# Second attention: the last item's probabilities multiplied before the new item's maxima on VectorE

## The chip, the cores and the metric

The kernel runs on one core of a Trainium2 chip. The time is device microseconds of one execution of the whole program. Of the kernel before there are three timed runs, with a median of 1680.32 us (1678.73 to 1683.52), and one profiled execution. TensorE is PE in the rows, VectorE DVE, ScalarE ACT, GpSimd POOL.

## What is computed

Two transformer blocks in float32 on one sequence of 512 tokens, width 1024. The first block has a retention mixer, an RWKV7 mixer, a cross attention and an MLP. The second block has four mixers beside each other, of four heads of 64 each, and a convolutional feed-forward part. The change is in the second block, in three of its four mixers, which the kernel computes in one stage:

```python
# diff attention: two softmaxes a head, subtracted
p = jax.nn.softmax(s, axis=-1)
w = p[:, :, 0] - lam * p[:, :, 1]
o = einsum('bhqk,bhkd->bhqd', w, v)
# forgetting attention: s + (cq[..., :, None] - cum[..., None, :]), causal
p = jax.nn.softmax(s, axis=-1)
# native sparse attention: three branches on one q, compressed keys (31),
# selected keys, window keys; each softmax(q k + bias) v, times its gate
o = g[:, 0] * o_c + g[:, 1] * o_s + g[:, 2] * o_w
```

The fourth, stick breaking attention, is done in the stage before.

## The kernel before, in words

Every engine has its program written out by hand, one function for each engine and stage, and waits on semaphores. The dense products (L389) run before and after the stage; inside it there are only four blocks of a last one, in steps 0 to 1, and nothing else is there to fill TensorE.

`mixer_items` lists 40 **items**. An item is one tile of 128 queries (t is 0 to 3) for a pair of heads, with keys up to w = 128 (t + 1). Items 0 to 15 are diff items (four **maps**: two softmaxes for two heads) and fox items (two maps) in the order d d f d f d f f, twice, with t = 3, 0, 2, 1 for each kind. Items 16 to 39 are the sparse attention, two maps each, in triples of one t (3, 0, 2, 1, twice): the compressed keys (w = 31), the selected and the window keys (w = 128 to 512).

A loop over n, the **step**, stands in each engine's function:

- TensorE, `mixers_pe`: `scores(n)` (L2406, one matmul a map into one of four PSUM banks, which waits until VectorE has read that bank four maps earlier); then `turn(n - 2)` (L2418, transposes of the probabilities, which wait for them and for the PSUM bank that ScalarE's `keep(n - 3)` empties); then `times_v(n - 3)` (L2431).
- VectorE, `mixers_dve`: `front(n)` (L2474, for each map one pass that adds the bias to the scores, writes them negated to a ring of 8 slots in SBUF and accumulates the minimum; it waits for the scores, for the transposes that read the slot before, and for the fox bias), then `back(n - 1)` (L2481 a reciprocal of the sums; L2483 a mask for w = 31; L2490 and L2495 the four multiplies of a diff item; L2502 or L2504 two multiplies of the others), which waits for the exponentials of item n - 1.
- ScalarE, `mixers_act`: `exps(n)` (L2526, one exponential a map with its sum, after that map's minimum), then `keep(n - 2)` (L2535, the transposed probabilities from PSUM to SBUF), now and then `keep_out(n - 4)` (L2541) and work for the next stage (`beside_mixers_act`: L2782, L2788, L2792).
- GpSimd, `fox_bias_pool`: the biases of the eight fox items (L2571, L2573), two fox items ahead.

So in one step VectorE takes the maxima of item n and afterwards multiplies the probabilities of item n - 1, whose exponentials ScalarE computed in the meantime. Four items are in flight. The small subtractions of `beside_mixers_dve` (L2807, four of them) stand at the end of a step.

Of the kernel before, what the change touches and what calls it, by code (L numbers as in the profile page):

```python
# [160 lines left out]
def build_program(nc, A, out):  # L161

    ctx = ExitStack()
    with ctx:
# [182 lines left out]
        def fill(steps, n):  # L347

            for _ in range(n):
                next(steps, None)  # L350
# [67 lines left out]
        def evac_steps(side, me, chunks):  # L418

            for ch in chunks:  # L420
                ahead = ch["index"] + 1
                while ahead < len(STREAM) and STREAM[ahead].get("kind"):
                    ahead += 1
                split_weights(side, me, ahead)
                if me == "dve" and ch.get("kind") == "modulation":
                    add_modulation(side, ch)
                for b in ch["blocks"]:
                    if units_of(b) == 2:
                        yield
                    if b["last"] and b["owner"] == me:  # L430
                        side.wait_ge(acc_done, b["acc"])
                        b["evac"](side, ps[0:b["m"], b["bank"], 0:b["n"]], bank_free[me], b["free"])
                    elif b["last"] and b["other"]:
                        b["other"](side, bank_free[b["owner"]], b["free"])
                    yield
# [1881 lines left out]
        def ring(j):  # L2317

            return yT[:, j, :] if j < 4 else SRING[:, j % 8, :]
# [71 lines left out]
        MIX = mixer_items()  # L2391
# [69 lines left out]
        def mixers_dve(v):  # L2461

            def front(it):
                for k, (_, _, bias) in enumerate(it["maps"]):
                    j = it["j0"] + k
                    v.wait_ge(mx_scores, j + 1)
                    if j >= 12:

                        v.wait_ge(mx_turned, 2 * MAP_ITEM[j - 8]["n"] + 2)
                    if it["kind"] == "fox":  # L2470
                        v.wait_ge(fox_bias, 2 * it["fox"] + k + 1)
                    r = j % 8

                    nc.vector.tensor_tensor_reduce(  # L2474
                        out=ring(j)[:, 0:it["w"]], in0=ps[:, j % 4, 0:it["w"]], in1=bias, scale=-1.0, scalar=3.0e38,
                        op0=ALU.add, op1=ALU.min, accum_out=MINS[:, r:r + 1]).then_inc(mx_shifted, 1)

            def back(it):
                n_maps, w, r, j0 = len(it["maps"]), it["w"], it["j0"] % 8, it["j0"]
                v.wait_ge(mx_exp, it["j0"] + n_maps)  # L2480
                nc.vector.reciprocal(RECS[:, r:r + n_maps], SUMS[:, r:r + n_maps]).then_inc(dve_order, 1)  # L2481
                if it["valid"] is not None:
                    nc.vector.tensor_tensor(SRING[:, r:r + 2, 0:w], SRING[:, r:r + 2, 0:w], it["valid"],  # L2483
                                            ALU.mult).then_inc(dve_order, 1)
                    v.count(dve_order)
                v.wait_ge(dve_order, v.count(dve_order))
                if it["kind"] == "diff":
                    for e in range(2):
                        p1 = ring(j0 + 2 + e)[:, 0:w]
                        nc.vector.tensor_scalar(p1, p1, RECS[:, r + 2 + e:r + 3 + e], NEG_LAM, ALU.mult,  # L2490
                                                ALU.mult).then_inc(dve_order, 1)
                    for e in range(2):
                        p = ring(j0 + e)[:, 0:w]
                        v.wait_ge(dve_order, v.count(dve_order))
                        nc.vector.scalar_tensor_tensor(out=p, in0=p, scalar=RECS[:, r + e:r + e + 1],  # L2495
                                                       in1=ring(j0 + 2 + e)[:, 0:w], op0=ALU.mult,
                                                       op1=ALU.add).then_inc(mx_probs, 1)
                    return
                for e in range(2):
                    p, rec = ring(j0 + e)[:, 0:w], RECS[:, r + e:r + e + 1]  # L2500
                    if it["gate"]:
                        ins = nc.vector.tensor_scalar(p, p, rec, it["gate"][e], ALU.mult, ALU.mult)  # L2502
                    else:
                        ins = nc.vector.tensor_scalar(p, p, rec, None, ALU.mult)  # L2504
                    ins.then_inc(mx_probs, 1)

            dense = evac_steps(v, "dve", v_tail)
            fill(dense, 1)
            for n in range(len(MIX) + 1):
                if n < len(MIX):  # L2510
                    front(MIX[n])
                if n:
                    back(MIX[n - 1])
                if n < 2:
                    fill(dense, n + 1)
                beside_mixers_dve(v, n)
# [286 lines left out]
        def beside_mixers_dve(v, n):  # L2803
            if n - 2 in MIX_SPLIT:
                k = MIX_SPLIT[n - 2]
                v.wait_ge(split_high, v.count(split_high))
                nc.vector.tensor_tensor(Y_LOW[:, k - 2, :], yT[:, k, :], Y_HIGH[:, k - 2, :].bitcast(F32),  # L2807
                                        ALU.subtract).then_inc(split_low, 1)
# [330 lines left out]
        @block.vector  # L3139
        def _(eng):  # L3140
            v = Side(eng, stage_sem)
            v.split = 0
            start_dve(v)
            front1_dve(v)
            invert_dve(v)
            v.stage_end()
            grams_dve(v)
            v.stage_end()
            scan_dve(v)
            v.stage_end()  # L3150
            w_out_dve(v)
            w_qkv_dve(v)
            v.stage_end()
            cross_dve(v)
            w_o_dve(v)
            mlp_dve(v)
            front_dve(v)
            mixers_dve(v)
            w_out_2_dve(v)
            evac_products(v, "dve", ffn)  # L3160
# [68 lines left out]
```

## Time and profile before

| what | value |
|---|---|
| three timed runs, median | 1680.32 us |
| the profiled execution, its own time | 1683.01 us |
| its span | 1681.2 us |
| PE busy, share of the span | 1610.1 us, 96% |
| DVE busy | 889.3 us, 53% |
| ACT busy | 660.7 us, 39% |
| POOL busy | 102.3 us, 6% |
| mean granted clock of TensorE | 0.991 |
| the stage with the 40 items | from 1151.9 to 1264 us of the span |

The profile is of one execution. Busy time is the time in which an engine had an instruction under way; TensorE's matmuls overlap, so a busy TensorE need not be at its peak. A release time is inferred from semaphores: behind a row, `[1.88 <-PE ps L2406]` says that the engine was idle for 1.88 us until an instruction of PE on line 2406 ended.

### The profile page before, as it was taken

The page shows a single profiled execution, that of the slowest core. Times are in us where ns is not written, and L with a number is a line of the kernel's source. Part 1 is how long each engine was busy: PE and PEld are TensorE (multiplying, and loading weights), DVE is VectorE, ACT ScalarE, POOL GpSimd, SP SyncE. Part 2 cuts the span into 40 slices and gives each one's busy share as a digit, 9 for nine tenths or more (in the row PEclk, how much of TensorE's full clock was granted, in tenths as well). Part 3 has the DMA queues.
Part 4 walks back from the last instruction along what each step waited for, and adds up shares of the span by engine and source line. Part 5 has one row for each costly group of instructions (what it writes and reads, how often), then busy time and mean ns, then how long its engine had stood idle before and what let it go on. Part 6 is the DMA issues. An engine that isn't in the chain of part 4 may idle for free.

```text
span 1681.2 us, 26254 instructions
## 1 busy us (share of the span) xinstructions
PE 1610.1 (96%) x11335; PEld 1288.7 (77%) x11335; DVE 889.3 (53%) x1384; ACT 660.7 (39%) x990; POOL 102.3 (6%) x125
## 2 busy tenths in 40 slices
PE   7999987899999999999999999999889999999998
PEld 5866767878896778888888778786558788888887
DVE  6454584516445364555455644537775655555544
ACT  3215932143534354333241334656774522222220
POOL 1300115000000000000000100003200000000000
PEclk9999999999999999999999999999899999999999
DMA  6612120005242345536453442321003233333222
GB/s 212 178 51 75 54 84 4 4 28 184 91 151 76 125 130 161 190 109 217 125 191 133 152 130 61 76 76 51 3 13 89 75 101 100 101 100 92 88 86 87
DMA packets 150694, 170.32 MB, mean 101 GB/s; under 512 B 14296, under 2 KB 111202, under 8 KB 150194
## 3 DMA queue, kind: packets, MB, share of 16 engines
q1 hardware_dynamic: 142424, 156.82, 29.6%
q10 hardware_dynamic: 8154, 11.81, 2.5%
q8 instruction: 90, 1.47, 0.4%
q14 instruction: 26, 0.21, 0.0%
HBM read 164.12 MB, written 6.33 MB: 101 GB/s over the span
## 4 chain that ended last, share of the span: by engine, by line
PE 83%; DVE 6%; ACT 5%; issue 2%; DMA 1%; POOL 1%; ACTq 0%; SPq 0%; DVEq 0%; POOLq 0%
PE ps L389 66%; PE ps L1255 3%; PE ps L1435 2%; DVE weights_low L412 1%; PE ps L2406 1%; PE ps L2418 1%; DMA sb_arena<-sb_arena 1%; PE ps L2431 1%; PE ps L2614 1%; PE ps L1661 1%; ACT sb_hT L2526 1%; PE ps L895 1%; PE ps L907 1%; ACT weights_high L409 1%; ACT sb_arena L672 1%
## 5 line engine op out<-in xcount | busy, mean ns | idle before, releaser
L389 PE MATMUL ps<-left_high,weights_high 128*128 128x512 f32 (+1 forms) x1016 | 404.1, 398 | 8.3 <-DVE left_low L694 3.1
L412 DVE TENSOR_TENSOR weights_low<-sb_weights_raw,weights_high 128x2048 fp32r<-128x2048 f32 (+1 forms) x118 | 265.2, 2248 | 258.2 <-ACT weights_high L409 258.1
L389 PE MATMUL ps<-left_low,weights_high 128*128 128x512 f32 (+1 forms) x1016 | 396.4, 390 | 0.0
L389 PE MATMUL ps<-left_high,weights_low 128*128 128x512 f32 (+1 forms) x1016 | 396.3, 390 | 0.0
L409 ACT CAST weights_high<-sb_weights_raw 128x2048 fp32r<-128x2048 f32 (+1 forms) x118 | 221.4, 1877 | 324.3 <-PE ps L389 282.7
L389 PEld LDWEIGHTS ps<-left_high,weights_high 128*128 128x128 f32 (+1 forms) x1016 | 190.3, 187 | 64.1 <-issue 13.2
L389 PEld LDWEIGHTS ps<-left_high,weights_low 128*128 128x128 f32 (+1 forms) x1016 | 190.5, 187 | 41.0
L389 PEld LDWEIGHTS ps<-left_low,weights_high 128*128 128x128 f32 (+1 forms) x1016 | 190.6, 188 | 40.4 <-issue 1.7
L389 PE MATMUL ps<-weights_high,hidden_high 128*128 128x512 f32 x432 | 169.0, 391 | 0.0
L389 PE MATMUL ps<-weights_high,hidden_low 128*128 128x512 f32 x432 | 168.2, 389 | 0.0
L389 PE MATMUL ps<-weights_low,hidden_high 128*128 128x512 f32 x432 | 168.1, 389 | 0.0
L389 PE MATMUL ps<-weights_high,left_high 128*128 128x256 f32 (+2 forms) x320 | 105.4, 329 | 1.6 <-DVE weights_low L412 1.2
L389 PE MATMUL ps<-weights_low,left_high 128*128 128x256 f32 (+2 forms) x320 | 103.9, 325 | 0.0
L389 PE MATMUL ps<-weights_high,left_low 128*128 128x256 f32 (+2 forms) x320 | 103.9, 325 | 0.0
L389 PEld LDWEIGHTS ps<-weights_high,hidden_low 128*128 128x128 f32 x432 | 81.1, 188 | 17.2
L389 PEld LDWEIGHTS ps<-weights_high,hidden_high 128*128 128x128 f32 x432 | 81.1, 188 | 16.7
L389 PEld LDWEIGHTS ps<-weights_low,hidden_high 128*128 128x128 f32 x432 | 81.1, 188 | 16.5
L1874 DVE TENSOR_TENSOR hidden_low<-sb_arena,hidden_high 128x512 fp32r<-128x512 f32 x54 | 37.3, 691 | 89.3 <-ACT hidden_high L1869 89.3
L389 PEld LDWEIGHTS ps<-weights_high,left_high 128*128 128x128 f32 x320 | 60.8, 190 | 10.5 <-issue 2.7
L389 PEld LDWEIGHTS ps<-weights_low,left_high 128*128 128x128 f32 x320 | 60.8, 190 | 5.5 <-issue 0.5
L389 PEld LDWEIGHTS ps<-weights_high,left_low 128*128 128x128 f32 x320 | 60.8, 190 | 5.1
L451 DVE SCALAR_TENSOR_TENSOR sb_arena<-sb_yT,sb_derived_cols,sb_arena 128x512 f32<-128x512 f32 x84 | 63.1, 751 | 3.0
(408 smaller groups left out, 2135.0 us busy)
## 6 DMA issues: line engine op xcount, KB each, us to landing
sb_weights_raw<-in_w_in SPq DMA_DIRECT2D x25, 1024.0 KB, 5.3
sb_yT<-in_ada_w SPq DMA_DIRECT2D x24, 1024.0 KB, 5.2
sb_weights_raw<-in_ffn_w_up SPq DMA_DIRECT2D x44, 512.0 KB, 5.0
sb_weights_raw<-in_mlp_w_up SPq DMA_DIRECT2D x16, 1024.0 KB, 6.2
sb_weights_raw<-in_mlp_w_down SPq DMA_DIRECT2D x16, 1024.0 KB, 7.8
sb_weights_raw<-in_ffn_w_down SPq DMA_DIRECT2D x10, 1024.0 KB, 5.0
sb_weights_raw<-in_xattn_w_kv SPq DMA_DIRECT2D x8, 1024.0 KB, 5.2
sb_weights_raw<-in_w_out SPq DMA_DIRECT2D x6, 1024.0 KB, 5.0
```

What stands on the lines that cost most here:

```text
L389: last = nc.tensor.matmul(o, lhsT, rhs, start=b["first"] and i == 0, stop=b["last"] and i == len(pairs) - 1)
L409: nc.scalar.copy(h[:, 0:n], raw[:, 0:n]).then_inc(w_high, 1)
L412: nc.vector.tensor_tensor(l[:, 0:n], raw[:, 0:n], h[:, 0:n].bitcast(F32), ALU.subtract).then_inc(w_low, 1)
L451: nc.vector.scalar_tensor_tensor(out=MOD_ACC, in0=w[:, k], scalar=C_ACT[:, kt:kt + 1], in1=MOD_ACC, op0=ALU.mult, op1=ALU.add).then_inc(do ...
L672: nc.scalar.activation(nm["shifted"][:, k, :], ps[:, k, :], ACT.Identity, scale=nm["gain"](k), bias=nm["shift"](k)).then_inc(norm_shifted, 1)
L895: nc.tensor.matmul(ps[:, 2 + n % 4, 0:w], KTt[b, p_, kt * P:(kt + 1) * P], QT[b, p_, kt * P:S], start=True, stop=True).then_inc(ret_scores, 1)
L907: last = nc.tensor.matmul(ps[64 * e:64 * e + 64, 6 + p_ % 2, kt * P:S], VR[:, kt, h * 64:(h + 1) * 64], SCO[:, (s - 2) % 3, e, 0:w], start ...
L1255: last = nc.tensor.matmul(ps[to, bank, c * 64:(c + 1) * 64], lhsT(b, u, c), rhs(b, u, c), start=True, stop=True)
L1435: last = nc.tensor.matmul(o_of(b), *own_pairs[i], start=i == 0, stop=i == len(own_pairs) - 1)
L1661: last = nc.tensor.matmul(ps[b, 6 + o % 2, q0:S], v_of(x), PT[0:m, buf, x, q0:S], start=grp["begins"] and x == 0, stop=grp["ends"] and x = ...
L1874: nc.vector.tensor_tensor(HIDL[part % 2][:, i, :], x, HIDH[part % 2][:, i, :].bitcast(F32), ALU.subtract).then_inc(ff_low, 1)
L2406: nc.tensor.matmul(ps[:, j % 4, 0:it["w"]], l, r, start=True, stop=True).then_inc(mx_scores, 1)
```

## The change

In VectorE's loop the two calls change places. From step 1 on, `back(n - 1)` comes first, and `front(n)` after it. Nothing else is changed: no instruction is added, removed or altered, and the programs of the other four engines are the same, row for row.

```diff
             for n in range(len(MIX) + 1):
+                if n:
+                    back(MIX[n - 1])
                 if n < len(MIX):
                     front(MIX[n])
-                if n:
-                    back(MIX[n - 1])
                 if n < 2:
                     fill(dense, n + 1)
                 beside_mixers_dve(v, n)
```

VectorE's order at the first sparse triple, before. ISA is the pass of `front` (128x512: selected or window keys of the last query tile; 128x31: compressed keys), the rows 128x1 its accumulator. The first rows are the maxima of item 17 (selected keys); the words in brackets are the semaphores that a row waits for.

```order
L2474 ISA sb_hT,sb_stat<-ps,sb_arena 128x512 [waits mix_probs_turned,mix_scores]
L2474 ISA sb_stat 128x1
L2481 RECIPROCAL sb_stat<-sb_stat 128x2 [waits mix_exp_ready]
L2483 TENSOR_TENSOR sb_hT<-sb_hT,sb_arena 128x2x31
L2502 TENSOR_SCALAR sb_hT<-sb_hT,sb_stat,sb_arena 128x31 [waits dve_order]
L2502 TENSOR_SCALAR sb_hT<-sb_hT,sb_stat,sb_arena 128x31
L2474 ISA sb_hT,sb_stat<-ps,sb_arena 128x512 [waits mix_probs_turned,mix_scores]
L2474 ISA sb_stat 128x1
L2474 ISA sb_hT,sb_stat<-ps,sb_arena 128x512 [waits mix_probs_turned,mix_scores]
L2474 ISA sb_stat 128x1
L2481 RECIPROCAL sb_stat<-sb_stat 128x2 [waits mix_exp_ready]
L2502 TENSOR_SCALAR sb_hT<-sb_hT,sb_stat,sb_arena 128x512 [waits dve_order]
```

The same place in the changed kernel:

```order
L2483 TENSOR_TENSOR sb_hT<-sb_hT,sb_arena 128x2x31
L2502 TENSOR_SCALAR sb_hT<-sb_hT,sb_stat,sb_arena 128x31 [waits dve_order]
L2502 TENSOR_SCALAR sb_hT<-sb_hT,sb_stat,sb_arena 128x31
L2474 ISA sb_hT,sb_stat<-ps,sb_arena 128x512 [waits mix_probs_turned,mix_scores]
L2474 ISA sb_stat 128x1
L2474 ISA sb_hT,sb_stat<-ps,sb_arena 128x512 [waits mix_probs_turned,mix_scores]
L2474 ISA sb_stat 128x1
L2481 RECIPROCAL sb_stat<-sb_stat 128x2 [waits mix_exp_ready]
L2502 TENSOR_SCALAR sb_hT<-sb_hT,sb_stat,sb_arena 128x512 [waits dve_order]
L2502 TENSOR_SCALAR sb_hT<-sb_hT,sb_stat,sb_arena 128x512
L2474 ISA sb_hT,sb_stat<-ps,sb_arena 128x512 [waits mix_probs_turned,mix_scores]
L2474 ISA sb_stat 128x1
```

Before, the reciprocal that waits for item 16's exponentials stood behind the maxima of item 17; now the maxima of item 17 are followed at once by the reciprocal that waits for the exponentials of item 17 itself, and the maxima of item 18 stand behind it.

## Rows read from the trace of the kernel before

**Rows 1.** Busy time in two stretches: items 2 to 15, items 16 to 39; columns: stretch, length, then per engine busy (instructions), then PEclk, DMA

```profile
1162.30:1206.60 44.30, 38.57 (x284) 23.96 (x282) 37.20 (x136) 32.66 (x109) 20.57 (x27) 0.85 0.00 1
1206.60:1262.30 55.70, 48.66 (x402) 29.77 (x402) 39.49 (x184) 43.30 (x159) 0.00 (x0) 0.97 0.04 11
```

**Rows 2.** Waits, 1162.3 to 1262.3 us: total, times, longest

```profile
ACT sb_hT L2526 <- DVE sb_stat L2474: 28.4, 25, 5.8
DVE sb_hT L2474 <- PE ps L2406: 17.4, 21, 3.0
```

**Rows 3.** Timeline of DVE, item 18's maxima and item 17's multiplies: start, length

```profile
1211.99 0.69 DVE L2474 CUSTOM_DVE_ANT_0 sb_hT<-ps,sb_arena 128x512 f32<-128x512 f32 x1 [0.40 <-PE ps L2406]
...
1212.61 0.69 DVE L2474 CUSTOM_DVE_ANT_0 sb_hT<-ps,sb_arena 128x512 f32<-128x512 f32 x1
...
1213.22 0.16 DVE L2481 RECIPROCAL sb_stat<-sb_stat 128x2 f32<-128x2 f32 x1
1213.42 1.00 DVE L2502 TENSOR_SCALAR sb_hT<-sb_hT,sb_stat,sb_arena 128x512 f32<-128x512 f32 x2
1214.33 0.20 DVE L2474 CUSTOM_DVE_ANT_0 sb_hT<-ps,sb_arena 128x31 f32<-128x31 f32 x1
```

**Rows 4.** Timeline of ACT, the exponentials of item 18

```profile
1212.73 0.72 ACT L2526 ACTIVATE sb_hT<-sb_hT,sb_stat 128x512 f32<-128x512 f32 x1
...
1213.45 0.70 ACT L2526 ACTIVATE sb_hT<-sb_hT,sb_stat 128x512 f32<-128x512 f32 x1
1214.06 0.18 ACT L2526 ACTIVATION_READ_ACCUMULATOR sb_hT<-sb_hT,sb_stat 128x1 f32 x1
```

**Rows 5.** Groups of instructions by line, 1162.3 to 1262.3 us: count, busy, mean ns, idle before

```profile
L2526 ACT ACTIVATE sb_hT<-sb_hT,sb_stat 128x384 f32<-128x384 f32 (+4 forms) x88 | 44.8, 511 | 28.7 <-DVE sb_stat L2474 28.4
L2474 DVE CUSTOM_DVE_ANT_0 sb_hT<-ps,sb_arena 128x384 f32<-128x384 f32 (+4 forms) x72 | 27.7, 422 | 18.4 <-PE ps L2406 15.9 <-PE ps L2418 1.7 <-issue 0.4
...
L2502 DVE TENSOR_SCALAR sb_hT<-sb_hT,sb_stat,sb_arena 128x31 f32<-128x31 f32 (+4 forms) x48 | 16.9, 394 | 0.9
...
L2495 DVE SCALAR_TENSOR_TENSOR sb_hT<-sb_hT,sb_stat 128x128 f32<-128x128 f32 (+3 forms) x14 | 7.5, 575 | 0.0
...
L2490 DVE TENSOR_SCALAR sb_hT<-sb_hT,sb_stat,sb_derived_cols 128x128 f32<-128x128 f32 (+3 forms) x14 | 6.9, 531 | 0.3
L2481 DVE RECIPROCAL sb_stat<-sb_stat 128x2 f32<-128x2 f32 (+1 forms) x39 | 6.3, 162 | 0.0
...
L2504 DVE TENSOR_SCALAR sb_hT<-sb_hT,sb_stat 128x512 f32<-128x512 f32 (+3 forms) x16 | 5.5, 384 | 0.3
...
L2483 DVE TENSOR_TENSOR sb_hT<-sb_hT,sb_arena 128x62 f32<-128x62 f32 x8 | 1.6, 202 | 0.0
```

**Rows 6.** Timeline of ACT, a copy for TensorE's next users, and DVE, which waits for it

```profile
1405.25 0.62 ACT L1869 CAST hidden_high<-sb_arena 128x512 fp32r<-128x512 f32 x1 [2.70 <-DVE sb_arena L2864]
...
1405.97 0.69 DVE L1874 TENSOR_TENSOR hidden_low<-sb_arena,hidden_high 128x512 fp32r<-128x512 f32 x1 [0.76 <-ACT hidden_high L1869]
```

**Rows 7.** Timeline of DVE: last dense block, item 1's multiplies, end of the last item

```profile
1161.34 0.42 DVE L475 COPY sb_arena<-ps 128x256 f32<-128x256 f32 x1 [2.24 <-PE ps L389]
...
1163.62 0.17 DVE L2481 RECIPROCAL sb_stat<-sb_stat 128x4 f32<-128x4 f32 x1
...
1165.16 0.55 DVE L2474 CUSTOM_DVE_ANT_0 sb_hT<-ps,sb_arena 128x384 f32<-128x384 f32 x1
...
1261.45 0.73 DVE L2502 TENSOR_SCALAR sb_hT<-sb_hT,sb_stat,sb_arena 128x256 f32<-128x256 f32 x2
```

**Rows 8.** Timeline of ACT in step 31, from its copies after the exponentials

```profile
1240.48 1.04 ACT L2535 COPY sb_hT<-ps 128x512 f32<-128x512 f32 x2
...
1241.89 1.07 ACT L2788 ACTIVATE sb_arena<-sb_yT 128x1024 f32<-128x1024 f32 x1
```

**Rows 9.** Timeline of PE: eight transposes at granted clock 0.5, and at 1.0

```profile
1187.60 1.93 PE L2418 MATMUL ps<-sb_consts,sb_hT 128*128 128x128 f32 x8
...
1216.32 1.09 PE L2418 MATMUL ps<-sb_consts,sb_hT 128*128 128x128 f32 x8
```

## The prediction

> **What bounds the kernel now.** I began with the page: TensorE is busy for 96% of the span, nearly all of it dense products, and none of these is touched. So the change can only be worth what it does to the stage of the 40 items. Next came the busy time by stretch [rows 1]. From item 2 to item 39 the stage takes 100.0 us, and no engine fills it: PE 87.2 (38.57 + 48.66), DVE 76.7 (37.20 + 39.49), ACT 76.0 (32.66 + 43.30). A stage in which three engines are each busy for three quarters or more and none all the time is bound by how they wait for each other. The waits say how [rows 2]: DVE stands idle 21 times, 17.4 us in all, for the scores of TensorE, and ACT 25 times, 28.4 us, for the maxima of DVE. No row has DVE waiting for ACT's exponentials. That absence is what the present order buys: when DVE comes to multiply item n - 1, it has just spent the maxima of item n on something else, and the exponentials are ready.
>
> The round trip through TensorE is the one that shows. Multiplies of item n - 2 release its transposes, behind these and behind times_v(n - 3) stand the scores of item n + 1 in TensorE's queue, and DVE needs them two steps later.
>
> **What the change does.** It changes no instruction, only DVE's order. The multiplies of item n - 1 come one front earlier, so the transposes, and with them the next scores, come earlier: the 17.4 us of waiting for scores should go. In return DVE now goes from the last maximum of item n - 1 straight to a reciprocal that needs the sum of item n - 1's last exponential, and the maxima of item n are queued behind that reciprocal. ACT cannot start item n's exponentials before those. DVE and ACT thus work in turn, and a closed loop arises with one item in it:
>
> first maximum of item n, then all its exponentials on ACT, then the way back to DVE, then the multiplies of item n, then the first maximum of item n + 1.
>
> Only the first maximum counts, since ACT is the slower of the two: at 512 columns an exponential takes 0.72 and 0.70 us [rows 4] and the second maximum starts 0.62 after the first [rows 3]. For an item of two maps and 512 columns the loop costs: from the start of the maximum (1211.99) to the exponential (1212.73) 0.74; exponentials to the end of the accumulator read (1214.24) 1.51; the way from ACT to DVE; reciprocal and multiplies (1213.22 to 1214.33) 1.11 [rows 3, 4]. The way from ACT to DVE is not shown in this stage, since DVE never waits there. Its nearest row is in the feed-forward part: a copy ends at 1405.87 and DVE starts at 1405.97 [rows 6]; I take 0.10, with 0.05 to 0.15 as the ends. That makes 3.46 us for the item.
>
> **The sum over items 2 to 39** (38 items, 88 maps) goes by the grouped rows [rows 5]:
>
> - Exponentials: 44.8 us, all 88 of them, and the tail of the last accumulator read of each item, 0.10 x 38 = 3.8. Together 48.6.
> - Way to DVE: 0.10 x 38 = 3.8.
> - First maxima: one for each item; the mean of a map is 0.42, the items of 128 to 512 columns weigh it up to 0.43, and 0.04 follows until ACT starts: 0.47 x 38 = 17.8. The other 50 maxima are hidden behind exponentials.
> - Reciprocals and multiplies: 16.9 + 7.5 + 6.9 + 6.3 + 5.5 + 1.6 = 44.7. Off this go item 1's, 1.54 (1163.62 to 1165.16, [rows 7]), and 0.07 an item, by which a multiply's end overlaps the next start (0.16 + 1.00 stand in a stretch of 1.11 with a gap of 0.04, [rows 3]): 2.7. Rest 40.5.
>
> Sum 110.7 us, 2.91 an item, where the trace has 100 us for the same items.
>
> Its start: the last dense block is copied by 1161.76, item 1's multiplies (1.54) now stand ahead of item 2's maxima, so these start at 1163.3 [rows 7]. Scores of item 2 are there by then.
>
> Two additions. **ACT's other copies** fit beside the loop in most steps: after its exponentials ACT has as long as DVE needs for the way, the multiplies and the next first maximum, 1.95 at 512 columns, and its copies take 1.04 [rows 8]. They don't fit after the compressed keys that follow 512 columns, where the output copy and other work come on top. In step 31 this is 2.48 us (1240.48 to 1242.96, [rows 8]), while DVE needs about 1.2 (way 0.10, reciprocal 0.16, mask 0.20, two narrow multiplies 0.4, a narrow maximum 0.3; the last two are estimates from below the means in rows 5). Over by 1.2. Step 19 has a copy of half the size in place of the 1.07: over by 0.7. I add 0.3 for small ones: 2.2.
>
> **TensorE** has the loop's time for scores, transposes and times_v. With all of them wide, eight transposes take 1.09 at full clock, and times_v and scores about the same each: 3.3 against the loop's 3.46, and narrow neighbours leave more. So at 2.4 GHz it is hidden. At the lower level, 1.2 GHz, the eight take 1.93 [rows 9], an item nearly 5.8: over by 2.3. Before, the granted clock was at 0.5 in three stretches of 6.8, 6.8 and 3.4 us here, which the means 0.85 and 0.97 show [rows 1] (0.15 x 44.3 and 0.03 x 55.7 are 8.3 us of lost clock, twice that at half clock). By rows, such a stretch costs nothing over narrow items and up to 2.7 over wide ones; three cost 0 to 8. Narrow items are the more frequent, so I take 1.0.
>
> The four subtractions of L2807 stand before the wait for exponentials in the new order too, and fall into it: nothing. GpSimd's biases are made two fox items ahead; the shortest such lead in the new order, item 4's maxima to item 7's, holds two whole items of the loop: nothing.
>
> **Forecast.** DVE's last multiply ends at 1163.3 + 110.7 + 2.2 + 1.0 = 1277.2 instead of 1262.2 (1261.45 + 0.73, [rows 7]): 15.0 us later. What follows needs the last item's copies and starts as much later, with nothing to make it up. The profiled execution takes 1683.0; it would take 1698.0. That execution lies 2.7 above the median of the timed runs, 1680.3; against the median I predict **1695.3 us**, 0.9% slower.
>
> **Rivals.**
>
> *The waits for scores go and nothing takes their place (faster).* For it: rows 2, the 17.4 us are real, and TensorE has the most busy time in both stretches. If TensorE alone bound the stage, it would end after 87.2 us instead of 100.0: 12.8 less, 1667.5. The Trainium skill says, on the page "Perfetto Trace Analysis", section "Identifying the Most-Contended Engine", to find the engine with the highest occupancy and to optimize this one first; by that rule this result is the one to expect of feeding TensorE earlier. The same section warns that matmul busy time is a poor measure of how near TensorE is to its limit. Against this rival: the loop is made of dependences, each with a measured length. It decides where an item's loop is shorter than the 2.6 us that an item takes now (100.0/38), and it is so only for 31 and 128 columns and some of 256. Chance 0.03.
>
> *Both cancel.* The loop's terms are taken from rows in which ACT and DVE disturb each other; if they were 10% shorter, the sum would be 99.6 and the time 1684. Still, narrow and wide items average 2.91, and the terms are sums of durations. Chance 0.04 for within 0.3% (about 5 us), which is roughly what a measurement of this kernel can tell from no change.
>
> *TensorE's clock.* Longer waits thin out TensorE's work, and the granted clock fell here already with shorter ones [rows 1]. If it stood at the lower level under all wide items (eight of 512 columns at 2.3, eight of 384 at about 1), 26 us would come on top: up to 1721. The Trainium skill, page "TensorE: Matmul & The Clock Gate", section "What's actually happening", calls the throttled state the default, which activity releases; by that the changed stage, with less activity per microsecond, would lose more clock than this one. The rows agree in so far as the clock falls in this stage and stays at 0.991 over the whole span. Against it: at the lower level TensorE's work gets denser, and before it came back each time. Chance 0.08 for a time above the range.
>
> The change does what it says: the order shown above puts the waiting reciprocal ahead of the maxima, so I give that rival nothing.
>
> **Numbers.** The forecast, slower by 9 to 24 us, has 0.85. Low end: no overhang of ACT, no clock term (11.8 us over 1680.3), less 1.6 for the spread of the runs below their median and 1.5 if the multiplies meet GpSimd less often: 1689. High end: the clock term at its full 8 and the way from ACT at 0.15: 1704. Slower by over 0.3%: 0.85 + 0.08 = 0.93; the same 0.04; faster 0.03.
>
> **What would show it.** After: waits of DVE's L2481 on ACT's L2526 in nearly every item, 1 us or more at 512 columns, some 30 us or more in all; DVE's waits of 17.4 us for L2406 nearly gone; ACT's waits for L2474 in nearly every item; DVE from item 2's first maximum to the last multiply 114 us; two starts of L2474 for wide items 3.4 to 3.5 apart in a row. It would be wrong if DVE's reciprocals don't wait, or if L2474 still waits for L2406 by 10 us or more (then TensorE, probably at 1.2 GHz, bounds it), or if the stage after 1277 takes a different time than before.

## The result, and the profile after

| what | before | after |
|---|---|---|
| three timed runs, median | 1680.32 us (1678.73 to 1683.52) | 1703.45 us (1702.53 to 1704.3) |
| the profiled execution, its own time / its span | 1683.01 / 1681.2 us | 1704.3 / 1702.5 us |
| PE busy | 1610.1 us, 96% | 1623.9 us, 95% |
| DVE / ACT busy | 889.3 / 660.7 us | 891.2 / 661.3 us |
| mean granted clock of TensorE | 0.991 | 0.981 |
| item 2's first maximum to the last multiply | 1162.39 to 1262.18, 99.8 us | 1163.75 to 1283.21, 119.4 us |

The changed kernel is slower by 23.1 us: ratio 1.0134, 95% interval 1.0116 to 1.0152. The forecast was +15.0, the range +8.7 to +23.7: the result lies inside the range, 0.6 us from its upper end. Measured from item 0's first maximum, the last multiply ends 110.28 us later before and 130.66 us later after. So 20.4 of the 21.3 us between the two profiled executions lie inside the stage.

The two stretches of [rows 1], items 2 to 15 and 16 to 39, in the changed kernel (busy time by stretch; after the engines PEclk, DMA share, GB/s):

```profile
1163.70:1216.50 52.80, 44.10 (x281) 27.75 (x279) 36.63 (x135) 33.34 (x110) 19.70 (x26) 0.77 0.01 1
1216.50:1283.30 66.80, 56.59 (x401) 35.57 (x399) 40.09 (x181) 43.16 (x156) 0.00 (x0) 0.82 0.03 9
```

DVE's and ACT's work is what it was, within 0.7 us in each stretch. The stretches grew by 8.5 and 11.1 us, and the granted clock went from 0.85 and 0.97 to 0.77 and 0.82. PE's busy time grew by 5.5 and 7.9 us with the same matmuls, which fits the lower clock. Read in stretches of 1 us, the changed stage stands at a clock of 0.50 in seven places, 47.6 us in all. Before it was three places and 17.0 us.

The waits of the changed kernel from 1163.6 to 1283.3 us, beside [rows 2] (total, times, longest):

```profile
ACT sb_hT L2526 <- DVE sb_stat L2474: 46.1, 37, 3.8
...
DVE sb_stat L2481 <- ACT sb_hT L2526: 30.1, 37, 1.2
...
PE ps L2418 <- ACT sb_hT L2535: 17.8, 19, 1.8
DVE sb_hT L2474 <- PE ps L2406: 8.5, 8, 2.7
```

The second line has no counterpart before. DVE's reciprocal waits for ACT in 37 of 38 items. ACT waits for DVE's first maximum in 35 of 38 (the other two of its 37 waits are for a third maximum, in two items of four maps). So the two work in turn. DVE's waits for scores fell from 17.4 us to 8.5. The third line is most of TensorE's idle time; this is the same line before (waits, 1162.3 to 1262.3 us):

```profile
PE ps L2418 <- ACT sb_hT L2535: 9.7, 16, 1.2
```

Here is one turn of the loop on DVE, item 29 at 512 columns (timeline, start and length; [rows 3] is the same piece before):

```profile
1250.69 0.69 DVE L2474 CUSTOM_DVE_ANT_0 sb_hT<-ps,sb_arena 128x512 f32<-128x512 f32 x1
...
1251.30 0.69 DVE L2474 CUSTOM_DVE_ANT_0 sb_hT<-ps,sb_arena 128x512 f32<-128x512 f32 x1
...
1252.97 0.17 DVE L2481 RECIPROCAL sb_stat<-sb_stat 128x2 f32<-128x2 f32 x1 [0.97 <-ACT sb_hT L2526]
1253.17 1.00 DVE L2502 TENSOR_SCALAR sb_hT<-sb_hT,sb_stat,sb_arena 128x512 f32<-128x512 f32 x2
1254.09 0.68 DVE L2474 CUSTOM_DVE_ANT_0 sb_hT<-ps,sb_arena 128x512 f32<-128x512 f32 x1
```

And the same turn on ACT (timeline):

```profile
1251.42 0.72 ACT L2526 ACTIVATE sb_hT<-sb_hT,sb_stat 128x512 f32<-128x512 f32 x1 [0.46 <-DVE sb_stat L2474]
...
1252.14 0.70 ACT L2526 ACTIVATE sb_hT<-sb_hT,sb_stat 128x512 f32<-128x512 f32 x1
1252.75 0.18 ACT L2526 ACTIVATION_READ_ACCUMULATOR sb_hT<-sb_hT,sb_stat 128x1 f32 x1
```

From maximum to maximum (1250.69 to 1254.09) it takes 3.40 us, with no wait for scores in it. The accumulator read ends at 1252.93 and the reciprocal starts at 1252.97: the way from ACT to DVE is 0.04 us here, where 0.10 was taken.

The other part of the time shows on TensorE, steps 20 and 21 (timeline of PE; the first row is the transposes of item 18), and in DVE's next maximum, that of item 21:

```profile
1227.58 1.97 PE L2418 MATMUL ps<-sb_consts,sb_hT 128*128 128x128 f32 x8
1229.48 1.98 PE L2431 MATMUL ps<-sb_hT,sb_arena 128*64 128x128 f32 x16
1231.38 0.65 PE L2406 MATMUL ps<-sb_arena 64*128 64x128 f32 x4
```

```profile
1232.07 0.29 DVE L2474 CUSTOM_DVE_ANT_0 sb_hT<-ps,sb_arena 128x128 f32<-128x128 f32 x1 [2.06 <-PE ps L2406]
```

Eight transposes take 1.97 us, as at half clock in [rows 9], and an item of 128 columns waits 2.06 us for its scores. Busy time of this stretch and of the one before it:

```profile
1218.00:1225.00 7.00, 4.95 (x41) 2.69 (x38) 4.63 (x15) 4.57 (x14) 0.00 (x0) 0.99 0.00 0
1225.00:1232.00 7.00, 7.00 (x44) 5.34 (x43) 2.88 (x17) 4.45 (x14) 0.00 (x0) 0.52 0.20 57
```

At a granted clock of 0.99 PE is busy for 4.95 of 7.00 us, and then it stands at 0.52, one of the chip's two levels (1.2 GHz), with PE busy all the time. The level fell after the time in which TensorE had gaps.

DVE's waits in front of its maxima lie almost wholly at such places. There are eleven, 11.1 us in all (8.5 for scores, 1.3 for transposes, 1.3 for what the profile doesn't name). Ten of these waits, 10.8 us, began while the clock stood at 0.50 or within 0.5 us of its return. The longest, with the clock of the stretch in front of it (timeline of DVE, busy time by stretch):

```profile
1280.68 0.42 DVE L2474 CUSTOM_DVE_ANT_0 sb_hT<-ps,sb_arena 128x256 f32<-128x256 f32 x1 [2.69 <-PE ps L2406]
```

```profile
1273.00:1279.00 6.00, 6.00 (x31) 3.84 (x30) 2.94 (x16) 3.29 (x12) 0.00 (x0) 0.50 0.02 4
```

### The profile page after: what moved, and what is told of

The parts are those of the page before. It is cut to its first block, busy times and chain, and to the rows that moved or that the text cites. A ratio compares the mean times of both kernels' runs of the same rounds, so it can differ in the third digit from the quotient of the medians.

```text
span 1702.5 us, 26254 instructions
## 1 busy us (share of the span) xinstructions
PE 1623.9 (95%) x11335; PEld 1299.3 (76%) x11335; DVE 891.2 (52%) x1384; ACT 661.3 (39%) x990; POOL 101.8 (6%) x125
## 4 chain that ended last, share of the span: by engine, by line
PE 83%; DVE 6%; ACT 5%; issue 2%; DMA 1%; POOL 1%; ACTq 0%; SPq 0%; DVEq 0%; POOLq 0%
PE ps L389 66%; PE ps L1255 3%; PE ps L1435 2%; ACT sb_hT L2526 2%; PE ps L2418 2%; PE ps L2406 1%; DVE weights_low L412 1%; DMA sb_arena<-sb_arena 1%; PE ps L2431 1%; PE ps L2614 1%; PE ps L1661 1%; PE ps L895 1%; PE ps L907 1%; ACT weights_high L409 1%; DVE sb_arena L858 1%
## 5 line engine op out<-in xcount | busy, mean ns | idle before, releaser
L2526 ACT ACTIVATE sb_hT<-sb_hT,sb_stat 128x128 f32<-128x128 f32 (+4 forms) x92 | 46.3, 504 | 48.9 <-DVE sb_stat L2474 48.9
```

Of the source, the lines that this page charges most:

```text
L2526: nc.scalar.activation(s, s, ACT.Exp, scale=-1.0, bias=MINS[:, r:r + 1], accum_out=SUMS[:, r:r + 1]).then_inc(mx_exp, 1)
```

## The experiments

The theory: the new order closes a loop of DVE and ACT in each item, worth some 14 us, and the rest is TensorE's clock. Its rivals: the loss sits at a few places only; TensorE binds; or the clock is all of it. Times are medians, with the ratio to the kernel before in the same session (medians 1679.42, 1679.88 and 1680.60 us in the three sessions).

### Half of the items each

`first_pairs` turns the order for the steps that multiply the diff and fox items; `first_sparse` has `n > 16` in its place.

```diff
             for n in range(len(MIX) + 1):
-                if n:
+                first = n <= 16
+                if n and first:
                     back(MIX[n - 1])
                 if n < len(MIX):
                     front(MIX[n])
+                if n and not first:
+                    back(MIX[n - 1])
```

> The new order in steps 1 to 16 only (the diff and fox items), the old one in the sparse attention. The theory (with the new order VectorE and ScalarE work in turn, item by item, and the sum of these loops is longer than the stage was) puts the loss on every item, so it divides: in the two profiles the first maximum of item 16 comes 9.3 us later against the first maximum of item 0 (63.98 for 54.71). Expected 1680.3 + 9.3 = 1689.6 us, and this run and the one with the sparse half alone add up to the whole loss. The rival (the loss is a loss of TensorE's clock, which needs the whole long stage to develop) expects less than half of it here, under 1685.

> The new order from step 17 on only (the sparse attention). The theory expects the rest of the loss: 20.4 us of the stage less 9.3 is 11.1, so 1691.4 us, with waits of the reciprocals of 0.66 to 0.97 us in this part alone. The rival as in the run before: under 1685.

Measured: the diff and fox items alone 1691.83 us, ratio 1.0064 (1.0041 to 1.0086), +12.4. The sparse ones alone 1689.45 us, 1.0059 (1.0041 to 1.0078), +10.0. The two add up to 22.4, the whole is 23.1. So neither half makes the loss alone, nor do the two halves make it by acting on each other. The split came out as 12.4 and 10.0 where 9.3 and 11.1 were expected. In the half that is turned the wait appears, and in the other it doesn't (waits of the sparse kernel, items 2 to 39; all 22 lie in the sparse half):

```profile
DVE sb_stat L2481 <- ACT sb_hT L2529: 17.3, 22, 1.5
```

### Only where VectorE stood waiting, and a middle way

`chosen` has `first = n in (9, 10, 39) or (n > 16 and n % 3 == 2)`, which are eleven steps (the expectation's count is one too high). `middle` takes half of an item's maxima ahead of the multiplies and half behind:

```diff
+                if n < len(MIX):
+                    front(MIX[n], slice(0, len(MIX[n]["maps"]) // 2))
                 if n:
                     back(MIX[n - 1])
                 if n < len(MIX):
-                    front(MIX[n])
+                    front(MIX[n], slice(len(MIX[n]["maps"]) // 2, None))
```

> The new order in twelve steps only in which the old kernel's VectorE stood waiting for scores or transposes while the exponentials of the item before were already there: steps 9, 10, 39 and those after a compressed-keys item (17, 20, 23, 26, 29, 32, 35, 38 of the sparse half; two or three of them were only nearly ready). The theory says that the order is bad only where the exponentials aren't ready, so here it gains what fitted into the waits: 1.5 to 2.5 us at steps 9 and 10, up to 0.7 at each of the others where the multiplies of the narrow item are 0.74 long: 1672 to 1679 us. A rival that blames the early multiplies themselves (they wake TensorE's transposes into the scores' way) expects 1683 or more.

> Multiplies of the last item between the halves of the new item's maxima: one map (of two) or two (of four), then the multiplies, then the rest. ScalarE then has the new item's first maps to work on while VectorE multiplies. By the theory the loop loses one of two exponentials: for two maps of 512 columns 0.70 + 0.10 + 1.11 + 0.65 = 2.6 us in place of 3.4, for 31 columns 1.3 in place of 1.8. That is less than the 2.6 an item took before on average for all but the widest, so TensorE's chain bounds again, and the multiplies come earlier by a half front than in the kernel before: 1672 to 1681 us. If it were not the loop but the earlier place of the multiplies, this would be about halfway, 1690.

Measured: `chosen` 1681.53 us, 1.001 (0.9998 to 1.0023), no gain where 1672 to 1679 us was expected: a miss too. Its rival's 1683 us or more didn't come either. In its profiled execution, the fastest of ten, it spares 4.1 us of waits for scores (13.3 in place of 17.4) and has 3.1 us of waits for exponentials in their place:

```profile
DVE sb_hT L2474 <- PE ps L2406: 13.3, 14, 2.0
DVE sb_stat L2481 <- ACT sb_hT L2529: 3.1, 4, 1.1
```

`middle` was a plain miss: 1701.78 us, 1.0137 (1.0105 to 1.0169), where a gain or nothing was expected. Its waits, 1162.3 to 1279.4 us:

```profile
ACT sb_hT L2528 <- DVE sb_stat L2474: 41.5, 47, 3.7
...
DVE sb_hT L2474 <- PE ps L2406: 30.2, 24, 4.0
...
PE ps L2418 <- ACT sb_hT L2537: 19.9, 28, 1.7
...
DVE sb_stat L2481 <- ACT sb_hT L2528: 4.0, 8, 0.8
```

The waits for exponentials are nearly gone, as meant, but those for scores grew from 17.4 to 30.2 us. ACT's timeline shows what the split did:

```profile
1245.88 0.72 ACT L2528 ACTIVATE sb_hT<-sb_hT,sb_stat 128x512 f32<-128x512 f32 x1 [0.52 <-DVE sb_stat L2474]
...
1247.23 0.72 ACT L2528 ACTIVATE sb_hT<-sb_hT,sb_stat 128x512 f32<-128x512 f32 x1 [0.53 <-DVE sb_stat L2474]
...
1247.95 0.62 ACT L2537 COPY sb_hT<-ps 128x256 f32<-128x256 f32 x2
```

And PE's, a little later:

```profile
1248.44 0.54 PE L2418 MATMUL ps<-sb_consts,sb_hT 128*31 128x128 f32 x2 [1.09 <-ACT sb_hT L2537]
```

The second exponential now waits for a maximum that stands behind multiplies. The copy to SBUF stands behind that exponential in ACT's queue, the transposes wait for the copy, and the next scores stand behind the transposes. My reading is that this longer loop over all three engines took the place of the two that were meant to be avoided. It rests on these rows; no run tested it by itself, and at a granted clock of 0.93 and 0.85 a part of the loss is the clock's.

### A shorter exponential

The loop says that every microsecond of exponentials counts in the new order. In this pair the exponentials of maps of 256 columns and more run over the last half of the columns only, with a fixed scale: half of these exponentials is left out.

```diff
-                    s = ring(j)[:, 0:it["w"]]
-                    nc.scalar.activation(s, s, ACT.Exp, scale=-1.0, bias=MINS[:, r:r + 1],
+                    short = it["w"] > P
+                    s = ring(j)[:, (it["w"] // 2 if short else 0):it["w"]]
+                    nc.scalar.activation(s, s, ACT.Exp, scale=-0.01 if short else -1.0,
+                                         bias=ONE if short else MINS[:, r:r + 1],
```

> The new order, and the exponentials of all maps of 256 columns and more run over the last half of the columns only (leaves out half of the exponentials of the wide maps, and takes a fixed scale and bias there). By the durations of the 512, 384, 256 and 128 column exponentials this takes 16 x 0.21 + 20 x 0.16 + 20 x 0.10 = 8.6 us off items 2 to 39. By the theory every exponential lies on the path of the new order: 8 to 9 us less than the new order's 1703.5, so 1694.5 to 1695.5. A rival that has TensorE as the bound of the stage expects 3 us or less.

> The same shortening in the kernel before (same parts left out). Its VectorE never waits for an exponential. The narrow form of the theory (exponentials are hidden there) expects 0 to 2 us less than before. A wider form, that came up with the split order: in the kernel before, the exponentials of item n + 1 stand ahead of ScalarE's copies of item n - 1, these hold up TensorE's transposes, and behind these stand the scores, a loop over two items that holds one item's exponentials: 4 us less, 1676.

Measured: in the changed order 1696.98 us, 1.0094 (1.0077 to 1.011), 6.5 us less than 1703.45 and 1.5 us above the expected 1694.5 to 1695.5. In the order before 1676.39 us, 0.9981 (0.9971 to 0.9991), 3.5 less. The changed order gains nearly twice as much, and its wait for exponentials falls from 30.1 us to this (waits of the changed order):

```profile
DVE sb_stat L2481 <- ACT sb_hT L2527: 23.8, 34, 1.5
```

So the exponentials are on the path there, by 6.5 of the 8 to 9 us expected. A part of the 6.5 us may be clock: the lost clock (1 less the granted clock, times the span) was 23.3 us on the mean of its runs and 26.7 without the edit. That the order before gains at all says that the exponentials are not fully off the path in it either. The 3.5 us fit the wider form of the expectation, a path through ACT's copies and TensorE's transposes, but no run tested that path by itself.

### TensorE kept busy

If the clock is the whole loss, filling TensorE's gaps removes it. Two pairs do so. `warm` puts up to two small matmuls (128x128x128) ahead of every score matmul, into columns of the same PSUM bank that nobody reads. `light` puts one ahead of the first score of each item that is narrower than 512:

```diff
+                    if k == 0 and it["w"] < S:
+                        c = it["w"] // P * P
+                        nc.tensor.matmul(ps[:, j % 4, c:c + P], ident, ident, start=True, stop=True)
```

> The new order, and ahead of each score matmul up to two more matmuls of 128 x 128 x 128 into the unused columns of its bank (their result is overwritten or never read), at most 0.25 us a map at full clock. If the 8 us that the prediction missed are TensorE's lower clock, which comes of its idle gaps, the granted clock of the stage rises from 0.77 and 0.82 to 0.9 or more, VectorE's waits for scores and transposes fall from 11 to under 6 us, and the time falls by 4 to 8, to 1695.5 to 1699.5. If the waits come of the length of TensorE's queue at any clock, they grow with it: 1704 or more.

> The same matmuls in the kernel before. Its clock is at 0.85 and 0.97 in the stage, so there is less to win (8 us of lost clock, of which the three stretches cost part) and TensorE's queue is on its path at every item: 1678 to 1688. The difference of the two kernels with these matmuls tells how much of the 23 us is clock: by the theory it falls to 15 or less.

`warm` was too much: 1729.49 us (1725.43 to 1739.94) with the new order and 1736.83 us (1727.77 to 1739.2) with the old, ratios 1.03 (1.0264 to 1.0336) and 1.0324 (1.0293 to 1.0355). Both lie far above their forecasts. In the profiled executions the clock was 0.99 and 0.97 from 1165 to 1280 us, PE was busy for 113.4 and 113.7 of the 115.0 us, and TensorE's queue became the bound. The other six executions had 0.986 to 0.994 over the whole span, so they lost more clock; where in the span isn't known, since only one execution of each is profiled. Group of the added matmuls in the new order, 1165 to 1280 us (count, busy us, mean ns, idle before):

```profile
L2408 PE MATMUL ps<-sb_consts 128*128 128x128 f32 x204 | 38.7, 307 | 0.0
```

It tells one thing all the same. DVE's waits for scores, new order and then old, over the same stretch:

```profile
DVE sb_hT L2477 <- PE ps L2409: 17.0, 23, 1.3
```

```profile
DVE sb_hT L2477 <- PE ps L2409: 32.9, 41, 2.1
```

Where TensorE is the bound, feeding it earlier isn't a loss any more; whether it is a gain these runs leave open, since their ranges overlap.

> The new order with one more matmul of 128 x 128 x 128 (0.2 us) ahead of the first score of each item under 512 columns, 30 of them, about 7 us more work in a TensorE queue that has 19 us of idle time in front of its transposes. Over the runs of the kernel before the time goes up by 0.55 us for each us of lost clock (1 less the granted clock, times the span); the new order lost 26.7 us, the kernel before about 9.8, so 9 of the 23 us would be clock. If the extra matmuls keep the clock up (lost clock under 15 us), the time falls to 1696 to 1700; if the lost clock doesn't fall or the wait is the queue's length, 1703 to 1710.

> The same 30 matmuls in the kernel before, where TensorE's queue lies on the path of most items: up to 7 us more than before, 1680 to 1687. By the theory the distance to the new order with the same matmuls falls from 23 to 14 us, since that is the part that the loop of VectorE and ScalarE makes.

`light` came out as forecast. It adds 32 matmuls (the expectations count 30). The new order takes 1699.32 us, 1.0113 (1.009 to 1.0136), 4.1 less than without the extra matmuls. That is at the edge of the noise: its four runs go from 1696.61 to 1704.48 us, the three without from 1702.53 to 1704.30. The old order takes 1683.89 us, 1.0019 (1.0007 to 1.0032), 3.3 more. Stretches of the new order with them, items 2 to 15 and 16 to 39:

```profile
1162.80:1213.40 50.60, 41.14 (x305) 26.00 (x304) 36.49 (x136) 33.13 (x110) 19.68 (x26) 0.97 0.00 1
1213.40:1275.70 62.30, 55.28 (x437) 34.99 (x437) 40.17 (x181) 43.08 (x155) 0.00 (x0) 0.97 0.03 10
```

The clock is back at 0.97 in both, and the stage takes 112.9 us in place of 119.4. (This is the fastest of four executions beside the slowest of three; the medians are 4.1 us apart.) The waits of the loop stay, and those for scores are nearly gone:

```profile
ACT sb_hT L2529 <- DVE sb_stat L2477: 40.0, 35, 4.0
DVE sb_stat L2484 <- ACT sb_hT L2529: 31.3, 37, 1.7
...
PE ps L2421 <- ACT sb_hT L2538: 14.8, 19, 1.4
```

The same stretches of the old order with the extra matmuls:

```profile
1164.90:1207.10 42.20, 36.93 (x306) 23.28 (x306) 37.17 (x137) 32.81 (x110) 20.56 (x27) 1.00 0.01 1
1207.10:1265.00 57.90, 53.96 (x438) 34.26 (x440) 39.49 (x183) 43.15 (x157) 0.00 (x0) 1.00 0.03 10
```

With the clock mostly kept up, the two orders are 15.4 us apart (1699.32 less 1683.89), against 23.1 without the extra matmuls. In the profiled executions the two stages are 12.8 us apart (112.9 less 100.1). So the loop costs time at a high clock too, and the clock isn't the whole loss. How large its part is, the pair tells only roughly. The 4.1 us that the new order got back are the clock's gain less what the extra matmuls cost there. That they cost as much there as in the old order isn't shown: TensorE's waits for copies are longer in the new order. And over all its runs the new order still lost more clock than the old one, 14.4 us on the mean against 7.9.

### The scores earlier, without the loop

The old order's waits for scores are real, and there is another way to them: TensorE issues the scores of item n + 1 ahead of the transposes of item n - 2, from item 17 on. `ahead_before` has it with the old order of DVE, `ahead_changed` with the new.

```diff
-                if n < len(MIX):
+                if n < 17:
                     scores(MIX[n])
+                if 16 <= n < len(MIX) - 1:
+                    scores(MIX[n + 1])
```

> The kernel before, and TensorE issues the scores of item n + 1 in step n, ahead of the transposes of item n - 2, in the sparse attention (from item 17 on; two maps an item, so the four banks suffice). The theory of what bounded the kernel before (a round trip: multiplies, transposes, times_v, then the scores that VectorE waits for; 17.4 us of waits, some 12 of them in this half) expects these waits under 4 us and the sparse half, now 55.6 us, at 48 to 51: 1673 to 1676 us. The rival (ScalarE's copies between the exponentials are the bound, and the scores only come late because nobody needs them earlier) expects the waits to change name and the time to stay within 1678 to 1682.

> The same in the new order. Here VectorE and ScalarE work in turn, so scores that are there earlier help only where VectorE still waited for them, 8.5 us in all, some 8 of them in this half and most of them at TensorE's lower clock. The theory expects up to 7 us less than 1703.5 and the loop untouched: 1696 to 1700, with the waits of the reciprocals still 17 us or more in this half. A rival that has the late scores as the cause of the loss expects it to fall to the level of the same edit in the kernel before.

Measured: 1671.26 us with the old order, ratio 0.9945 (0.9925 to 0.9965), 9.3 us faster than the kernel before, more than the 1673 to 1676 us expected, and the fastest whole kernel of this study. With the new order 1696.78 us, 1.0088 (1.0063 to 1.0113), 6.7 us less than 1703.45, as forecast. The stretches of the old order with it, in its profiled execution (own time 1670.02):

```profile
1160.40:1201.50 41.10, 33.55 (x284) 20.41 (x286) 37.04 (x136) 32.40 (x109) 20.53 (x27) 1.00 0.01 2
1201.50:1248.00 46.50, 45.00 (x394) 27.79 (x390) 39.08 (x184) 42.28 (x157) 0.00 (x0) 1.00 0.04 13
```

Its waits:

```profile
ACT sb_hT L2528 <- DVE sb_stat L2476: 13.8, 11, 5.8
...
PE ps L2418 <- ACT sb_hT L2537: 5.7, 11, 1.1
...
DVE sb_hT L2476 <- PE ps L2406: 3.6, 8, 0.7
```

The sparse half shrank from 55.7 us to 46.5, DVE's waits for scores in the stage from 17.4 to 3.6 us, and PE's for copies from 9.7 to 5.7. PE is now busy for 45.00 of the 46.50 us of the sparse half: there TensorE is close to being the bound. The first half, where nothing is changed, was 3.2 us shorter too, at a clock of 1.00 in place of 0.85: that part is the clock of this execution, and the median of six is the better figure.

With the new order, the waits for the exponentials stand as before (waits of `ahead_changed`, 1162 to 1275 us):

```profile
DVE sb_stat L2483 <- ACT sb_hT L2528: 30.6, 35, 1.9
```

Scores that come earlier take away DVE's waits for scores, but not the loop, in which they have no part. The distance between the two orders even grew, to 25.5 us.

## Why the prediction was right, and where its sum was off

**Direction and mechanism: right.** All of the signs named beforehand are there but two: waits of L2481 for L2526 in 37 of 38 items, 30.1 us where "some 30 us" was said, 0.97 us at 512 columns where 1 or more was said; ACT's waits for L2474's first maximum in 35 items; wide items 3.40 us apart (3.4 to 3.5 was said, 3.46 taken). The first that failed: DVE's waits for L2406 are 8.5 us, not nearly gone, close to the 10 us at which TensorE at 1.2 GHz was to be held the bound. The second: the stage took 119.4 us, not 114.

**The sum by its terms.** DVE waited in the changed stage for 8.5 us for scores, 1.3 for transposes and 1.3 for what the profile doesn't name, 11.1 in all. Without these the 38 items took 119.4 - 11.1 = 108.3 us, where 110.7 + 2.2 = 112.9 were forecast. The sum for the loop was 4.6 us too large and the waits for TensorE were 11.1 us where 1.0 was forecast. The two errors have opposite signs. That they partly cancel is luck: with the loop at its measured size and the 1.0 us for TensorE, the forecast would have been +10.4 us, where 23.1 were measured.

- *Reciprocals and multiplies:* 44.7 less item 1's 1.54, so 43.2 of busy time, was forecast; measured 43.2 (16.9 + 7.1 + 6.4 + 6.4 + 4.8 + 1.6). Single rows moved: L2504 took 7.1 us where it took 5.5, L2490 4.8 where it took 6.9 with item 1's in it.
- *Exponentials:* 44.7 us, 44.8 forecast.
- *The way from ACT to DVE:* 0.04 in place of 0.10 wherever it was read, 2.3 us less over 38 items.
- *ACT's overhang:* 2.2 us forecast. In step 31, where 1.2 of it was put, ACT's copies end late enough to delay item 32's first exponential by 0.45 us. In step 19, where 0.7 was put, item 20's comes 0.27 us late. Item 26's is the third that didn't wait for DVE, and it isn't late. So about 0.7 us of this term occurred.
- *L2807's subtractions:* nothing, as said. One of them fills part of a reciprocal's wait, which is 0.37 us there and not 0.97.

**The step that failed is the TensorE term, 1.0 us.** The prediction read three stretches at half clock before, gave them 0 to 8 us, and chose 1.0, because such a stretch costs nothing over narrow items. It took their number over unchanged, though the change stretches TensorE's work. In the changed kernel (1 - 0.77) x 52.8 + (1 - 0.82) x 66.8 = 24.2 us of clock are lost in the stage, against 8.3 before. Of DVE's 11.1 us of waits, 10.8 began at the half clock or just behind it, as shown above. That all of them would go at the full clock isn't shown: in the new order of the `light` pair, at 0.97, 2.7 us of waits for scores were left. What one microsecond of lost clock goes with, the runs of the kernel before give: over 46 of them, in all sessions, the time rises by 0.56 us for each microsecond of lost clock (1 less the granted clock, times the span), with a correlation of 0.82. The kernel before loses 10.8 us on the mean, the changed one 26.7. By that slope, which is an estimate where it is carried over to another kernel, the clock makes 15.8 x 0.56 = 8.8 of the 23.1 us, and 14.3 remain for the loop, which the forecast put at 14.0. The 46 runs lost between 5.0 and 20.2 us, so 26.7 lies outside them, and a correlation doesn't say by itself which of the two makes the other. The `light` pair gives 15.4 us between the orders, or 12.8 between the profiled stages, with the open points named there. Taken together, and as an estimate, the loop makes some 12 to 15 us and the clock most of the rest.

The loop's size is less exact than 14.3 against 14.0 looks: its two small terms, way and overhang, were some 4 us too large in the changed execution (2.3 and 1.5). With the clock kept up the stage took 112.9 us, which is 110.7 + 2.2, but in it stand 2.7 us of waits for scores and the extra matmuls.

**The rivals.** *Faster, TensorE alone bounds:* wrong here. Its condition, an item's loop shorter than the time that TensorE leaves, holds in the `warm` pair, and there the new order was not slower. The Trainium skill's advice, page "Perfetto Trace Analysis", section "Identifying the Most-Contended Engine", to optimize the engine with the highest occupancy first, pointed at TensorE; by itself it didn't tell which order feeds it. TensorE's scores issued earlier did gain 9.3 us, and VectorE's multiplies made earlier lost 23.1. *Both cancel:* wrong for the whole, but it is what `chosen` does on eleven steps. *TensorE's clock:* wrong as to the whole loss and right in kind. It was priced at 26 us on top, with a chance of 0.08, and came at some 8 to 11 by the estimates above. The Trainium skill, page "TensorE: Matmul & The Clock Gate", section "What's actually happening", calls the throttled state the default and activity what releases it; here the traces agree, 0.77 and 0.82 in the sparser stage against 0.97 with extra matmuls.

**What stays open.** The exact share of the clock: the same kernel's runs differ by some 4 us to each side, and no run held the clock at 1.00 with nothing else changed. And why `middle` loses as much as it does.

## What to carry to other kernels

When two engines hand an item back and forth, write down the loop that their in-order queues close: here one instruction's place, a reciprocal that waits for this item's own exponentials with the next item's maxima behind it, left DVE and ACT only one item to work on at a time and cost some 12 to 15 us of 100. A wait is best removed at the engine that is late without touching the others' slack: the same waits for scores cost 23 us when VectorE was turned around for them and gave back 9 when TensorE issued the scores earlier. And a stage that gets longer with the same matmuls has to be priced at the clock that it may lose, not at the clock that it had.

## What the runs showed of the hardware

- TensorE's granted clock fell to half in a stage in which its waits for ACT's copies (L2418 for L2535) were at most 1.8 us each (17.8 us in 19). Before, with 9.7 us in 16 waits of at most 1.2, the stage lost a third as much clock (8.3 us against 24.2).
- With 32 extra 128x128x128 matmuls, which no result needs, the granted clock of the changed stage was 0.97 in the profiled execution, where it had been 0.77 and 0.82. The median time was 4.1 us lower, with overlapping ranges. The same matmuls in the old order cost 3.3 us.
- The spread of a kernel's runs by some 4 us to each side goes with this clock (correlation 0.82 over 46 runs): a run at a granted clock of 0.996 over the whole took 1675.17 us, one at 0.988 took 1684.85.
- From the end of ACT's accumulator read to the start of the DVE instruction that waits for it 0.04 us pass (1252.93 to 1252.97).
